# Light experts of a mixture-of-experts layer loaded as whole rows, with blocks of two lengths placed in a ring by a table

## The reference

```python
def swiglu(h, w_gate, w_up, w_down):
    return (jax.nn.silu(h @ w_gate) * (h @ w_up)) @ w_down

def moe_swiglu(h, w_router, b_router, w_gate, w_up, w_down):
    ...
    gates = jnp.sum(jax.nn.one_hot(top_i, N_EXPERTS) * top_w[..., None], axis=-2)   # top 2 of 8
    for e in range(N_EXPERTS):
        out = out + gates[..., e:e + 1] * swiglu(h, w_gate[e], w_up[e], w_down[e])
```

## Time and profile before

| | us |
|---|---|
| median of 3 runs | 1721.28 |
| the profiled execution | 1721.49 |
| its span (first to last instruction) | 1719.8 |
| first weight load of the experts is issued | 1025.0 |
| PE starts on the last block | 1707.2 |
| last results are written | about 1717 |

### The profile page before, as it was taken

How to read it: one execution, slowest core, us unless ns; L and a number is a source line. 1 busy time by engine, 2 the same in 40 slices (tenths; PEclk the granted TensorE clock), 3 DMA queues, 4 the chain that set the end, 5 groups by cost and what they waited for, 6 DMA issues and landing times.

```text
span 1719.8 us, 25435 instructions
## 1 busy us (share of the span) xinstructions
PE 1625.6 (95%) x10722; PEld 903.4 (53%) x10722; DVE 647.6 (38%) x1501; ACT 354.6 (21%) x766; POOL 73.3 (4%) x147
## 2 busy tenths in 40 slices
PE   6999999989999999998997979999999999999985
PEld 3665544368888864443785764334434433343432
DVE  4987972474545521507589362000100010001001
ACT  4334452221101100003546342000100000000001
POOL 2210100000000030000011000000000000000000
PEclk9999999989999999998999979999999999999998
DMA  8503633443333153226143319999999999999997
GB/s 314 159 14 111 242 109 125 162 119 77 98 99 89 47 89 96 73 98 245 50 124 100 98 50 412 411 412 405 412 413 411 400 412 413 409 406 410 410 411 285
DMA packets 186064, 396.31 MB, mean 230 GB/s; under 512 B 34371, under 2 KB 104619, under 8 KB 170842
## 3 DMA queue, kind: packets, MB, share of 16 engines
q1 hardware_dynamic: 180576, 391.23, 61.8%
q0 software_dynamic: 4112, 3.34, 1.3%
q10 hardware_dynamic: 1258, 0.07, 0.0%
HBM read 389.36 MB, written 1.05 MB: 227 GB/s over the span
## 4 chain that ended last, share of the span: by engine, by line
PE 88%; DVE 4%; DMA 3%; ACT 2%; SPq 1%; issue 1%; ACTq 0%; DVEq 0%
PE ps L1073 85%; PE ps L1076 3%; DMA ring<-in_w_in_dram 1%; DVE norms L1987 1%; DMA ring<-in_moe_w_down_dram 1%; SPq L579 1%; DMA ring<-in_moe_w_gate_dram 1%; DVE aT L1995 0%; DVE work L2004 0%; ACT dg L741 0%; ACT work L732 0%; ACT work L733 0%; DVE hT L2009 0%; ACT work L848 0%; DVE aT L2221 0%
## 5 line engine op out<-in xcount | busy, mean ns | idle before, releaser
L1073 PE MATMUL ps<-ring,work 128*32 128x256 f32 (+5 forms) x3368 | 404.2, 488 | 11.3 <-DMA ring<-in_moe_w_down_dram 7.0
L1073 PEld LDWEIGHTS ps<-ring,work 128*32 128x32 f32 (+2 forms) x3368 | 155.4, 118 | 250.8 <-issue 209.0
L1073 PE MATMUL ps<-work 128*64 128x64 f32 (+11 forms) x2348 | 232.5, 326 | 9.1 <-DVE work L2271 5.1
L1073 PE MATMUL ps<-work,ring 128*128 128x512 f32 (+1 forms) x656 | 237.0, 514 | 1.3 <-DVE work L2303 1.3
L1073 PE MATMUL ps<-aT,ring 128*128 128x256 f32 (+1 forms) x800 | 235.3, 443 | 2.9 <-ACT aT L805 2.2
L2458 DVE TENSOR_TENSOR work<-work,ps 128x768 f32<-128x768 f32 (+5 forms) x27 | 18.8, 706 | 525.3 <-PE ps L1073 525.3
L1073 PEld LDWEIGHTS ps<-work 128*64 128x64 f32 (+5 forms) x2348 | 157.7, 150 | 74.5 <-issue 58.8
L1073 PEld LDWEIGHTS ps<-aT,ring 128*128 128x128 f32 x800 | 152.3, 192 | 72.6 <-issue 54.4
L1073 PE MATMUL ps<-aT,work 128*128 128x256 f32 (+6 forms) x1148 | 185.4, 466 | 4.5 <-DMA aT<-in_moe_w_down_dram 4.5
L1073 PEld LDWEIGHTS ps<-work,ring 128*128 128x128 f32 x656 | 124.5, 190 | 106.4 <-issue 98.5
L1073 PEld LDWEIGHTS ps<-aT,work 128*32 128x32 f32 (+2 forms) x1148 | 105.3, 143 | 70.7 <-issue 48.4
(11 more groups left out here) (360 smaller groups left out, 1291.2 us busy)
## 6 DMA issues: line engine op xcount, KB each, us to landing
ring<-in_moe_w_up_dram SPq DMA_DIRECT2D x55, 1024.0 KB, 16.3
ring<-in_moe_w_down_dram SPq DMA_DIRECT2D x51, 1024.0 KB, 15.6
ring<-in_w_ada_dram SPq DMA_DIRECT2D x23, 2048.0 KB
ring<-in_moe_w_gate_dram SPq DMA_DIRECT2D x37, 1024.0 KB, 15.2
ring<-in_moe_w_up_dram SPq DMA_DIRECT2D x28, 768.0 KB, 16.7
aT<-in_moe_w_gate_dram SPq DMA_DIRECT2D x17, 1024.0 KB, 15.6
aT<-in_moe_w_down_dram SPq DMA_DIRECT2D x17, 1024.0 KB, 17.3
ring<-in_moe_w_gate_dram SPq DMA_DIRECT2D x18, 768.0 KB, 16.3
```

Of the source, the lines that this page charges most:

```text
L1073: return pe.matmul(o, lhs, rhs, start=start, stop=stop)
```

## The change

1. The experts of ranks 4 to 7 are no longer cut into chunks: each is one item with all 2816 columns. The items are now (a, 0), (b, 0), (a, 1), (a, 2) for the first three pairs (a, b), then (3, 0), (3, 1), (3, 2), (7, 0): 16 items.
2. A block of gate or up of a light expert is 128 rows of 11,264 B, one for each partition (11 KB in a partition, 1.375 MB in all); there are 8 for each matrix. All other blocks stay as they were. There are 248 blocks.
3. For ranks 4 to 6 the down rows are paired in 10 blocks of 11, where before they were paired in 8 of 11; rank 7 stays paired throughout.
4. `aT` and `ring` are now one tensor `arena` of 80 KB in each partition. A table made when the kernel is built places each block: at the next place in the arena that is long enough, going round, or, for a block of 8 KB, in `norms` or `Sg` where that is free earlier. `after[n]` is the last block that used any byte of that place (and not less than n-16, since there are 16 semaphores for landings); SP waits for it before it issues block n.
5. `hs` and `hTs` have one copy instead of two. ACT's copy to `hTs` of item i waits until the down blocks of item i-1 are used (before: of item i-2).
6. The sums of a light expert take PSUM banks 0, 1 and 7 for gate and 2, 3 and 4 for up. PE waits for the results of the pair before to be copied from bank 7 ahead of a gate that uses it.
7. The spreads of the pairs stay in the up of the first item of the next pair. `spread_alone` and `carry` of rank 3 are now both in the up of the single tiny item, one step behind each of its 8 blocks.

```diff
-        items = [(r, c) for pair in PAIRS[:-1] for c in range(NC) for r in pair]
-        items += [(r, c) for r in PAIRS[-1] for c in range(NC)]
+        items = []
+        for a, b in PAIRS[:-1]:
+            items += [(a, 0), (b, 0), (a, 1), (a, 2)]
+        items += [(LAST, c) for c in range(NC)] + [(TINY, 0)]
...
+        def rows_per_block(i):
+            return 2 if big(i) else 1
...
-        def row_pairs(i):
-            return width(i) == 1024 or heavy(i) or tiny(i)
+        def row_pairs(i, d):
+            if not big(i):
+                return tiny(i) or d < FN // 2 - 1
+            return width(i) == 1024 or heavy(i)
...
-        def home(n):
-            m = n % n_blocks
-            return m % EARLY if m < LATE_FROM else (m - EARLY) % NBUF
...
+        for n, size in enumerate(sizes):
+            need_cells = size // cell
+            if head + need_cells > ARENA // cell:
+                head = 0
+            options = [(max(taken["arena"][head:head + need_cells]), 0, "arena")]
+            if size == 2 * D:
+                options.append((taken["norms"][0], 1, "norms"))
+                if n >= LATE_FROM:
+                    options.append((taken["Sg"][0], 2, "Sg"))
+            prev, _, where = min(options)
+            if where == "arena":
+                places.append((where, head * cell))
+                taken[where][head:head + need_cells] = [n] * need_cells
+                head += need_cells
+            else:
+                places.append((where, 0))
+                taken[where][0] = n
+            after.append(max(prev, n - NSEM))
...
-                        if i >= 2:
-                            act.wait_ge(sem("block_used"), b0 + down_end[i - 2])
+                        if i:
+                            act.wait_ge(sem("block_used"), b0 + down_end[i - 1])
...
+                    if not big(i):
+                        if bank == 0 and not tiny(i) and p0 + i // PER:
+                            for g in range(2):
+                                pe.wait_ge(sem(f"y_ready{g}"), 2 * (p0 + i // PER))
+                        for k in range(KC):
+                            pe.wait_ge(block_in(n), landed_at(n))
+                            ...
+                                for part, o in enumerate((0, 1, 7) if bank == 0 else (2, 3, 4)):
+                                    lo, hi = 512 * part, min(512 * part + 512, FE // 2)
+                                    for g in range(2):
+                                        last = mm(ps[HP * g:HP * g + HP, o, 0:hi - lo], lhs,
+                                                  b[:, 0, FE // 2 * g + lo:FE // 2 * g + hi], k == 0, k == KC - 1)
+                            last.then_inc(sem("block_used"), 1)
+                            n += 1
+                            between(k)
```

More of the change, by code:

```diff
@@ new lines, in block_in, with landed_at @@
+        def block_in(n):
+            return sem(f"block_in{n % NSEM}")
+        def landed_at(n):
+            return 16 * (n // NSEM + 1)
+        def wblock(n):
+            where, at_ = places[n % n_blocks]
+            size = sizes[n % n_blocks]
+            if where == "arena":
+                b = arena[:, at_:at_ + size]
+            else:
+                b = norms[:] if where == "norms" else Sg.rearrange("p i r s -> p (i r s)")
+            return b.rearrange("p (k n) -> p k n", k=1 if size == FE else 2)
@@ L568, in experts, with load @@
                 n, expert = ph * n_blocks, {}
-                def load(n, i, src, paired=False):
+                def load(n, src, order):
                     m = n - ph * n_blocks
-                    if m == LATE_FROM:
+                    if places[m][0] == "Sg" and after[m] < LATE_FROM:
                         sp.wait_ge(sem("gates_turned"), 4 * ph + 4)
-                    elif m >= EARLY:
-                        sp.wait_ge(sem("block_used"), n + 1 - (EARLY if m < LATE_FROM else NBUF))
+                    if after[m] >= 0:
+                        sp.wait_ge(sem("block_used"), ph * n_blocks + after[m] + 1)
@@ L576, in load, with load_in @@
                     elif ph:
                         sp.wait_ge(sem("block_used"), n_blocks)
-                    order = "e (p k) n -> p (e k) n" if paired else "e (k p) n -> p (e k) n"
-                    sp.dma_start(wblock(n)[:, :, 0:src.shape[2]], src.rearrange(order, p=P))\
-                        .then_inc(sem(f"block_in{home(n)}"), 16)
+                    sp.dma_start(wblock(n)[:, :, 0:src.shape[-1]], src.rearrange(order, p=P)).then_inc(block_in(n), 16)
+                def load_in(n, i, w):
+                    f0, width_ = chunk(i)
+                    rows = P * rows_per_block(i)
+                    for d in range(blocks_in(i)):
+                        load(n, w[0, bass.ds(expert[items[i][0]], 1), rows * d:rows * d + rows, f0:f0 + width_], "e (k p) n -> p (e k) n")
+                        n += 1
+                    return n
@@ new lines, in load_down @@
+                def load_down(n, i):
+                    f0, w = chunk(i)
+                    one = moe_down[0, bass.ds(expert[items[i][0]], 1), f0:f0 + w, :]
+                    split = not big(i) and not tiny(i)
+                    for d in range(w // 256):
+                        if not split:
+                            src = one[:, 256 * d:256 * d + 256, :]
+                        elif d < FN // 2 - 1:
+                            at_ = FE // 2 * (d // 5) + 256 * (d % 5)
+                            src = one[:, at_:at_ + 256, :]
+                        if split and d == FN // 2 - 1:
+                            load(n, one.rearrange("e (h r) n -> r (e h) n", h=2)[FE // 2 - P:FE // 2], "p k n -> p k n")
+                        else:
+                            load(n, src, "e (p k) n -> p (e k) n" if row_pairs(i, d) else "e (k p) n -> p (e k) n")
+                        n += 1
+                    return n
@@ L582, in experts @@
                 for i in range(NI):
-                    r, c = items[i]
-                    f0, w = CHUNK[c]
+                    r = items[i][0]
                     if r not in expert:
                         expert[r] = sp.value_load(by_rank[0:1, r:r + 1], min_val=0, max_val=NE - 1)
[L587 to L590, removed]
+                    n = load_in(n, i, moe_gate)
@@ L591, in experts @@
                     if i:
[L592 to L604, removed]
+                        n = load_down(n, i - 1)
@@ L606, in _ @@
+                    n = load_in(n, i, moe_up)
+                load_down(n, NI - 1)
             sp.wait_ge(sem("ftok_turned"), 4)
@@ L2451, in experts @@
                             copy_y(ended)
-                        for q in range(3):
+                        for q in range(3 if i < ALONE else 4):
                             add(ended, q)
```

208 lines of the change are left out of this document (113 added, 95 removed).

## The result

| | before | after |
|---|---|---|
| median | 1721.49 us (6 runs) | 1729.3 us (6 runs, 1729.14 to 1730.32) |
| ratio, 95% interval | | 1.0049 [1.0036, 1.0062] |
| span of the profiled execution | 1719.8 us | 1728.5 us |
| first landing to last landing of the experts' weights | 677.1 us | 685.6 us |

The change makes the kernel 8.4 us slower by the ratio. The forecast was 1726.2 us (1715 to 1734), slower with 0.64.

What follows compares the result with a forecast made beforehand. The DMA stream of the experts' weights, not PE, was taken to set the end. 1721.5 us - 9.5 (fewer packets) + 14.2 (stalls at four places) = 1726.2 us, 0.3% slower, range 1715 to 1734.

Steps and rivals of the forecast that it cites:

- The bound: Experts' weights: the DMA stream, beginning at 1025.0 and carrying 277 MB, sets the end, though PE is busy 95%.
- The gain: Gate and up rows of 11,264 B in one packet instead of three, plus paired down blocks: 9.5 us saved.
- no better than its pieces: Rival: a long packet takes as long as its three pieces, leaving some 12.5 us of stalls; 1733.6 us, chance 0.08.
- First place: Rank 4's gate, blocks 9 to 14: loads wait for PE's unchanged releases; stalls sum to 4.2 us.
- Third place: Rank 5's gate, blocks 135 to 139: 20.4 us of cover against a backlog of 20.8; stalls sum to 7.0 us.
- Fourth place: Rank 7's gate, block 221: 18.0 us of cover; old backlog of 10.5 gives no stall; 1.5 us taken.
- Second place: Rank 6's up, block 87: 17.0 us of cover; old backlog of 15.0 gives 0.6 us; 1.5 taken.
- the backlog swings more: New order's longer runs of one kind make PE's delay from landing to release vary more; buffers hold less than the swing.
- The formula: Stall equals backlog (landing to release) + 2.6 us lead - cover (transfers between a block and the one it waits for).
- Nothing for PE, ACT and DVE: Other engines: same matmuls and turns; single `hs` and `hTs`, bank 7 and moved spreads cost nothing.
- the fed stream: Rival: backlog is small whenever long blocks come, so only the 9.5 us saving remains; 1712.0 us, chance 0.13.
- gain and stalls cancel: Rival: each stall lets PE catch up, backlogs 3 us below the old, 7.8 us of stalls; 1719.8 us, chance 0.18.

## Why the prediction was right in sign and 3 us short

**The bound** held: the end moved with the last landing (8.6 us, the span 8.7), and PE's busy time didn't change (1621.9 for 1625.6). Undone from either side, by more arena or by less backlog, much of the loss went: 24.8 us of lost time became 18.3 and 13.2.

**The gain** was forecast at 9.5 us and is 9.5 by the medians. Windows with long blocks alone show 424 GB/s, the lower edge of what I had named; cutting the packets costs 9.2 us. A long block's 3.39 us is the value of the line through the earlier trace rows. The rival "no better than its pieces" is out: 424 against 407 in the same window. What the Trainium skill says of the ports' ceiling ("DMA: Bandwidth & Descriptors", Where 436 GB/s comes from) isn't contradicted by any window: the highest rates that I find in the changed trace are 435 GB/s over 10 us (1429.8 to 1439.8) and 429 over 20 us (1427 to 1447), where the packets at a window's edge are counted whole.

**First place**: the releases came as read from before: block 9 is issued at 1049.32 and block 10 at 1054.48 in the changed trace. That 4.2 was forecast and 4.2 measured is in part luck. The forecast counts all that is lost, and that is 5.6; 4.2 is what is left when the 1.3 are taken off that the kernel before loses at the same blocks. And the single terms differ: 0.4, 1.8, 0, 0.4 and 1.6 were forecast for blocks 9 to 13, and they are 0.5, 1.1, 1.4, 1.0 and 0.7.

**Third place**: the first two terms came out (block 135 2.9 for 3.0; blocks 136 and 137 together 3.3 for 3.4). The term for blocks 138 and 139 was 0.6 and is 2.1, or 4.0 with one engine's lag. The releases came 3.8 us apart as forecast, but the lead was too small: I had taken 5.8 us from issue to landing for a long block with nothing ahead of it, from one load of 1 MB, and block 10 took 5.9, but block 137 6.1, block 135 6.3 and block 138, issued while block 137 was ending, 7.0. The 16 engines finish block 138 over 1.8 us; why they do, no run shows.

**Fourth place**: 2.4 for 1.5. Here a step failed: I had read the backlog of rank 3's middle chunk, 10.5, from the old order. In the new one five chunks of 96 slots (rank 2's last two and rank 3's three) stand in a row, where the old one has rank 3's three behind a light chunk; the backlog is 15.5. But by my own formula even that gives only 15.5 + 2.6 - 18.0 = 0.1 at block 221, where 1.5 were lost, 0.7 of them by one engine that landed behind the other 15. So 1.5 for this place was a guess that came near, and most of the 2.4 isn't explained by the backlog.

**Second place**: 1.8 for 1.5, and again not for the reason given. The backlog at block 81 is 13.6, less than the 15.0 of before, which by the formula leaves no stall at block 87; 0.8 were lost there and 1.0 at block 76, rank 6's gate, where I had placed none. The backlog rose above the old one at the fourth place only (20.1 for 20.8 at the third), so that "the backlog swings more" held for one place of three.

**The formula**, backlog + 2.6 - cover, is borne out where the stream is empty on all engines (blocks 135 to 137), and the experiments show that cover and backlog both move the loss. It gives too little where long blocks are issued one by one and the engines finish them apart.

**What I left out**: the engines don't finish together. 1.3 us more is lost to single engines that fall behind than in before. The terms 0.3 + 1.3 + 0.9 + 1.3 make the 3.8 us between 14.2 and 18.0.

**Nothing for PE, ACT and DVE** held as far as the traces show: from 1055 to 1650 PE waits for no other engine, and from 1030 to the end for ACT and DVE 1.3 us in all. No run has the single `hs` and `hTs` or the new PSUM banks alone. PE did wait for DMA before 1650, as I had said it should.

**Slips in my arithmetic**: 1715 is four fifths of the way from the forecast to the fed stream (11.2 of 14.2 us), not two thirds. And with backlogs 3 us below the old ones the stalls at the third place are 3.4 + 0.3 + 0.3 = 4.0, not 3.6, which makes that sum 8.2 and its time 1720.2. Neither bears on the outcome.

**The rival "gain and stalls cancel"** rested on stalls relieving the later ones. No run shows much of that. With half of rank 0's work the third place closes, and the fourth stays about as deep, some 12 us earlier as the whole kernel is (349 GB/s from 1604 to 1625, where after has 368 from 1616 to 1640). With cut packets 5 to 7 of 9.2 us come back, but there the cover is longer too, so that this isn't relief by stalls alone.

## What to carry to other kernels

In a stream that is fed through a ring, count how many microseconds of transfers lie between a block and the load that takes its place, and compare that with the consumer's backlog at its peak plus the time that a load needs before its data come. In this kernel longer blocks in the same memory shortened the first, and the new order raised the second at one place of three. A gain in packet size comes out whole only where the first stays above the second: 8 KB rows with the old ring and order gave 4.7 of 4.7 us, 11 KB rows with whole experts gave 9.5 and lost 18. And test a loss of this kind from both sides, by more cover and by less backlog, before blaming the order.

## What the runs showed of the hardware

The time of a packet is linear up to 11,264 B: windows of one size give 402, 409 to 411, 421 and 424 GB/s for 3072, 4096, 8192 and 11,264 B. Instruction loads seem to take their turn on the same engines. In the trace of before, 16 KB packets of 1.1 us begin at 1159.9, 1386.7, 1500.3 and 1602.1, each while the block of one of the four steps (53, 148, 193, 236) travels; at each step 15 engines finish as before, and one 1.4 to 1.5 us behind them. Such packets come some 40 times in the stream, and the others leave no step; that they fall on engines that are ahead fits, but isn't shown. Here is the rate of before and then of after over the 8 us in which each stream ends (40 slices; a packet is counted whole where it begins, so that single slices jump):

```profile
GB/s 410 369 369 328 246 369 246 205 287 205 246 287 164 287 287 123 328 205 205 287 164 205 287 164 205 246 205 164 246 164 164 205 0 0 0 0 0 0 0 0
```

```profile
GB/s 492 246 574 369 328 573 369 369 573 246 492 573 205 328 369 82 246 287 82 205 164 82 164 123 82 123 123 82 41 41 0 0 0 0 0 0 0 0 0 0
```

Before, the engines finish over more than six microseconds (the first at 1700.8, the last at 1707.1); after, with stalls shortly ahead of the end, over 3.5. In the kernel before with 13 buffers, where the dip of slice 32 is gone (408 for 400 GB/s), the spread is 8.2 us and the time is the same. So in these runs a stall first cost the engines that were ahead, and a short one didn't reach the end.
